# Whole transfers for x and the first weight strip, and the first strip's products by turns of two token tiles

## The reference

```
def first_block(x, pre_mix_w, w_in, ...):
    ...
    h = rmsnorm(x, pre_mix_w[l])
    proj = h @ w_in[l]
    o0 = 0
    q_a = proj[..., o0:o0 + DA_QK] ...
    k_a = proj[..., o0:o0 + DA_QK] ...
```

## Time and profile before

| | |
|---|---|
| median of 3 runs | 753.26 us |
| the profiled execution | 753.9 us |
| its span in the profile | 752.2 us |
| PE busy | 745.2 us, 99% |
| VectorE, ScalarE, GpSimd busy | 480.9, 402.2 and 54.4 us |
| bytes read from memory | 132.61 MB |

### The profile page before, as it was taken

One profiled execution on the slowest core, in us unless ns is written; L12 is line 12 of the kernel. 1 busy time (PEld: TensorE's weight loads), 2 busy tenths in 40 slices (PEclk: granted clock), 3 DMA queues, 4 the chain that ended last, 5 costly groups with the idle time before them and its releaser, 6 DMA issues.

```text
span 752.2 us, 10167 instructions
## 1 busy us (share of the span) xinstructions
PE 745.2 (99%) x3847; PEld 618.6 (82%) x3847; DVE 480.9 (64%) x742; ACT 402.2 (53%) x607; POOL 54.4 (7%) x127
## 2 busy tenths in 40 slices
PE   9999999999999999999999999999999999999997
PEld 7887877888888888888898888888888888888886
DVE  5576766666956665774376877576865575566633
ACT  5646766544744444554368555676345455455422
POOL 1100100000460000000023000200002000000000
PEclk9999999999999999999999999999999999999999
DMA  8855454555656656546476373444464565555541
GB/s 317 269 184 212 137 173 136 191 171 179 220 172 196 192 167 201 196 157 206 127 237 200 110 240 118 126 154 129 147 216 154 190 202 165 193 192 174 195 140 57
DMA packets 57231, 134.34 MB, mean 179 GB/s; under 512 B 7831, under 2 KB 13278, under 8 KB 57182
## 3 DMA queue, kind: packets, MB, share of 16 engines
q1 hardware_dynamic: 56528, 132.16, 54.1%
q10 hardware_dynamic: 654, 1.53, 0.6%
HBM read 132.61 MB, written 1.05 MB: 178 GB/s over the span
## 4 chain that ended last, share of the span: by engine, by line
PE 98%; DMA 1%; DVE 0%; SPq 0%; ACT 0%; POOL 0%; issue 0%; ACTq 0%; POOLq 0%
PE acc L1113 87%; PE aux L1038 4%; PE aux L1216 1%; PE aux L1178 1%; PE aux L1251 1%; DMA x<-in_x_dram 1%; PE aux L1197 1%; PE acc L1104 1%; PE aux L1326 1%; PE aux L1241 0%; PE aux L1104 0%; PE aux L1356 0%; PE aux L1366 0%; PE aux L1341 0%; PE aux L1303 0%; PE aux L1306 0%
## 5 line engine op out<-in xcount | busy, mean ns | idle before, releaser
L1113 PE MATMUL acc<-weights_high,h_high 128*128 128x512 f32 (+1 forms) x720 | 229.3, 394 | 0.0
L1417 DVE SCALAR_TENSOR_TENSOR weights_low<-weights_raw,gain_columns,weights_high 128x1024 fp32r<-128x1024 f32 (+3 forms) x189 | 218.5, 1189 | 15.2 <-ACT weights_high L682 15.1
L1113 PE MATMUL acc<-weights_high,h_low 128*128 128x512 f32 (+1 forms) x720 | 224.3, 387 | 0.0
L1113 PE MATMUL acc<-weights_low,h_high 128*128 128x512 f32 (+1 forms) x720 | 223.9, 387 | 0.0
L682 ACT ACTIVATE weights_high<-weights_raw,gain_columns 128x1024 fp32r<-128x1024 f32 (+3 forms) x188 | 194.6, 1074 | 19.8 <-DMA weights_raw<-in_w_in_dram 11.7
L1113 PEld LDWEIGHTS acc<-weights_low,h_high 128*128 128x128 f32 x720 | 134.4, 188 | 27.6
L1113 PEld LDWEIGHTS acc<-weights_high,h_low 128*128 128x128 f32 x720 | 134.3, 188 | 27.5 <-DVE h_low L1436 0.4
L1113 PEld LDWEIGHTS acc<-weights_high,h_high 128*128 128x128 f32 x720 | 130.7, 188 | 25.4 <-issue 1.9
L1414 DVE TENSOR_TENSOR weights_low<-weights_raw,weights_high 128x1024 fp32r<-128x1024 f32 x68 | 81.0, 1220 | 35.9 <-ACT weights_high L682 35.7
L682 ACT ACTIVATE weights_high<-weights_raw 128x1024 fp32r<-128x1024 f32 x68 | 69.7, 1057 | 48.1 <-DMA weights_raw<-in_ffn_w_down_dram 22.6
L738 ACT ACTIVATE silu_tmp<-acc,stats 128x512 f32<-128x512 f32 (+1 forms) x24 | 15.7, 654 | 88.4 <-PE acc L1113 88.4
(11 more groups left out here) (269 smaller groups left out, 637.4 us busy)
## 6 DMA issues: line engine op xcount, KB each, us to landing
weights_raw<-in_w_in_dram SPq DMA_DIRECT2D x59, 512.0 KB, 5.1
weights_raw<-in_w_gate_dram SPq DMA_DIRECT2D x44, 256.0 KB, 3.4
weights_raw<-in_w_up_dram SPq DMA_DIRECT2D x44, 256.0 KB, 4.0
weights_raw<-in_w_down_dram SPq DMA_DIRECT2D x22, 512.0 KB, 4.6
weights_raw<-in_ffn_w_gate_dram SPq DMA_DIRECT2D x44, 256.0 KB, 3.3
weights_raw<-in_ffn_w_up_dram SPq DMA_DIRECT2D x44, 256.0 KB, 4.1
weights_raw<-in_ffn_w_down_dram SPq DMA_DIRECT2D x22, 512.0 KB, 4.8
weights_raw<-in_w_out_dram SPq DMA_DIRECT2D x16, 512.0 KB, 4.6
```

The source lines that it names most:

```text
L1113: i = nc.tensor.matmul(acc[:, 2 * t + b, 0:width], lhs[:, k0, sl], w[:, u % RING, base + d:base + d + width], start=(kt == 0 and n == 0), ...
L1417: i = nc.vector.scalar_tensor_tensor(lo[:, u % RING, c], raw[:, u % RING, c], gcol[:, g:g + 1], hi[:, u % RING, c].bitcast(F32), ALU.mult, ...
```

## The change

Four edits, all of them in the first microseconds:

- x comes in two transfers of 512 KB, one for each tile, in place of four of 256 KB, and both are issued ahead of strips 1 to 3. Strip 0 comes in one transfer of 512 KB on ScalarE's queue in place of two halves on two queues. ScalarE still makes its high part in two halves.
- The transposes of the identity are 4 in place of 8.
- A new function `first_products` writes the twelve matmuls of strip 0 for both tiles. The list's own steps for them are skipped.
- VectorE makes the high and low part of strips 0 and 1 of tile 0 first (`first_strips(0, 1, "mix_first")`) and those of strips 2 and 3 later, after tile 1's low part (`rest_of_first`).

```diff
-    out.append(do("warm", 8))
-    run("qk_a", [1, 1, 2, 4], {(0, 0): [do("norm_turn", "mix", 1, 0)], ...
+    out.append(do("warm", 4))
+    run("qk_a", [1, 1, 2, 4], {(0, 0): [do("norm_turn", "mix", 1, 0), do("rest_of_first")], ...
...
-            load_x(0, 0)
-            sp.dma_start(raw[:, 0, 512:1024], dram["w_in"][0, 0:P, 512:1024]).then_inc(*tick("raw_loaded0", 0, 16))
-            load_x(1, 0)
+            load_x(0)
+            load_x(1)
             weights(1)
             weights(2)
             weights(3)
-            load_x(0, 1)
-            load_x(1, 1)
...
-            act.dma_start(raw[:, 0, 0:512], ins["w_in"][0, 0:P, 0:512]).then_inc(*tick("first_loaded", None, 16))
+            act.dma_start(raw[:, 0, :], ins["w_in"][0, 0:P, 0:1024]).then_inc(*tick("first_loaded", None, 16))
...
+            def first_products():
+                def passes(t, lhs, w):
+                    for b in range(2):
+                        c = slice(512 * b, 512 * b + 512)
+                        if t == 0 and lhs is hT[0]:
+                            pe.wait_ge(*at("high_ready" if w is hi else "low_ready", (0, 0) if b else "left"))
+                        i = nc.tensor.matmul(acc[:, 2 * t + b, :], lhs[:, 0, t * P:(t + 1) * P], w[:, 0, c],
+                                             start=(lhs is hT[0] and w is hi), stop=False)
+                    return i
+                pe.wait_ge(*at("turned_high_vec", "mix_first"))
+                passes(0, hT[0], hi)
+                pe.wait_ge(*at("turned_low", "mix_first"))
+                passes(0, hT[1], hi)
+                step("norm_turn", "mix", 1, 0)
+                pe.wait_ge(*at("turned_high", ("mix", 1, 0)))
+                passes(1, hT[0], hi)
+                passes(0, hT[0], lo)
+                pe.wait_ge(*at("turned_low", ("mix", 1, 0)))
+                passes(1, hT[1], hi)
+                passes(1, hT[0], lo).then_inc(*tick("weights_used", 0))
...
+            def first_strips(k, bank, key):
+                high, low = (part[:, k:k + 2, 0:P] for part in hT)
+                src = aux[bank][:, 0:2 * P].rearrange("p (k s) -> p k s", k=2)
+                dve.wait_ge(*at("turned", key))
+                signal(nc.vector.tensor_copy(high, src), "turned_high_vec", key, True)
+                nc.vector.tensor_tensor(low, src, high.bitcast(F32), ALU.subtract).then_inc(*tick("turned_low", key))
```

More of the change, by code:

```diff
@@ L219, in timeline @@
     out.append(("ahead", 1))
-    out.append(do("warm", 8))
-    run("qk_a", [1, 1, 2, 4], {(0, 0): [do("norm_turn", "mix", 1, 0)], (0, 2): [do("norm_turn", "mix", 0, 1)],
+    out.append(do("warm", 4))
+    run("qk_a", [1, 1, 2, 4], {(0, 0): [do("norm_turn", "mix", 1, 0), do("rest_of_first")], (0, 2): [do("norm_turn", "mix", 0, 1)],
                             (1, 2): [do("norm_turn", "mix", 1, 1)], (1, 3): [do("stats", "mix", 0)],
@@ L577, in _, with load_x @@
             dram = ins
-            def load_x(t, b):
-                sp.dma_start(x[:, t, 512 * b:512 * b + 512], dram["x"][0, t * P:(t + 1) * P, 512 * b:512 * b + 512])\
-                    .then_inc(*tick(f"x_loaded{t}_{b}", None, 16))
+            def load_x(t):
+                sp.dma_start(x[:, t, :], dram["x"][0, t * P:(t + 1) * P, :]).then_inc(*tick(f"x_loaded{t}", None, 16))
             def bc(ap, n=P):
@@ L671, in advance @@
                             .then_inc(*tick("high_ready", "left"))
-                        act.wait_ge(*at("raw_loaded0", 0))
                         nc.scalar.activation(hi[:, 0, 512:1024], raw[:, 0, 512:1024], ACT.Copy, scale=gcol[:, 0:1])\
@@ L1089, in product @@
                 for n, (lhs, w) in enumerate(passes):
-                    if u == 0 and t == 0 and lhs is xl:
-                        step("norm_turn", "mix", 1, 0)
                     if t == 0 and w is lo:
@@ L1135, in step @@
                         if tag == "mix":
-                            pe.wait_ge(*at(f"x_loaded{t}_{b}"))
+                            pe.wait_ge(*at(f"x_loaded{t}"))
                         elif tag.startswith("merged"):
@@ L1389, in _ @@
             for st in steps:
-                if st == ("do", "norm_turn", "mix", 1, 0):
+                if st in (("do", "norm_turn", "mix", 1, 0), ("mm", "qk_a", 1, 0, None)):
+                    continue
+                if st == ("mm", "qk_a", 0, 0, None):
+                    first_products()
                     continue
@@ L1602, in step @@
                         if (tag, t, b) == ("mix", 0, 0):
[L1603 to L1614, removed]
+                            first_strips(0, 1, "mix_first")
                             continue
@@ L1617, in step @@
                                    0.5 if tag.startswith("merged") else 1.0)
+                elif kind == "rest_of_first":
+                    first_strips(2, 0, ("mix", 0, 0))
                 elif kind == "gain_turn":
```

## The result

The changed kernel takes 757.04 us in the median of 4 runs (756.43 to 758.81), the kernel before 753.25: a ratio of 1.0049, 95% interval 1.0037 to 1.0062. I had forecast 754.4, no change, and a range up to 756.2. The chances had 0.38 on slower, 0.22 of it on the mechanism that turned out to be the largest part.

A forecast was written before the change was run, and what follows sets the result against it. PE, 98% of the chain, was taken to bound the kernel. Landing L = 6.1 plus 5.35 us put strip 1's first product at 11.45 against 10.36, 1.1 us later: 753.26 becomes 754.4 us, range 753.3 to 756.2.

The forecast's parts named there:

- What bounds the kernel: Whole kernel: PE is 98% of the chain, so a change in the opening only moves the start of its gapless streaming.
- The transfers: Opening loads: 1.05 MB instead of 0.79 ahead of the first product; strip 1 taken to land at 9.5 us.
- L: Landing of x tile 0 and strip 0, both whole: taken as 6.1 us, between bounds 5.5 and 7.4.
- rival 1: Opening transfers: bytes come no faster in whole rows, L = 7.4, 2.4 us later, 755.7 us; chance 0.16.
- rival 3: Opening transfers: cold start was a matter of many small packets, L = 5.5, 0.5 us later, 753.8 us; chance 0.14.
- I let it be in by L: Gain columns' row, behind strip 0 on ACT's queue: assumed landed by L, with no time of its own.
- L + 1.45: Opening on PE: the second product's time, after ScalarE makes strip 0's high part in 1.34 us from L.
- From the second product on: Opening on PE: three products, tile 1's transposes and eight more products, to strip 1's first product at L + 5.35.
- VectorE's queue and strip 1's low part: Strip 1's low part, queued behind VectorE's moved pair: 12.43 us against PE's need at 12.37, adding under 0.1 us.
- The clock: Opening on PE: idle from about 4.5 to 6.1 us, then every product at 0.23 us.
- rival 2: Opening on PE: clock rises later after the idle gap, 755.1 to 757.3 us, most likely 755.9; chance 0.22.
- 1.1 us: Strip 1's first product on PE: 11.45 us against 10.36, a delay nothing later takes up.

The follow-up runs named there:

- e6: The changed kernel with the gain row's transfer issued ahead of strip 0's on ScalarE's queue, still 7 zero products: 760.53 us.
- e5: The changed kernel with 11 zero products in place of 7 and the gain row's transfer ahead of strip 0's on ScalarE's queue: 756.41 us.
- e1: The changed kernel with 11 zero products in place of 7 at PE's start: 755.71 us.
- e10: e1 with tile 1's transposes put back ahead of tile 0's activation low pass: 755.26 us.
- e7: e3 with 11 zero products in place of 7 (whole transfers, old order): 755.12 us.
- e9: e1 with the gain row's transfer issued first on SP's queue instead of second on ScalarE's: 755.38 us.
- e12: The old order with the whole transfers, 11 zero products and the gain row first on SP's queue: 754.74 us.
- e2: The kernel before with 3 zero products in place of 7: 755.14 us.
- e3: The kernel before with the whole transfers of x and strip 0 alone: 756.25 us.
- e8: The kernel before with strip 0 whole behind the gain row on ScalarE's queue, x still in halves: 756.23 us.

## Why the prediction was wrong, step by step

- **What bounds the kernel.** Right: the loss lies between the start and strip 1's first product (4.5 of 4.9 us in the profiles); the rest, 0.4 us, is the strip's first products before the clock rose. From 20 us on PE is idle for 5.6 us in all, before and after, and nothing was taken back.
- **The transfers.** Right in the landings, in part by luck. L was 5.8 to 6.0 against 6.1, x tile 1 at 7.3 (7.4), strip 1 at 8.6, better than the 9.5 taken. But the counts of bytes behind these figures are not what the trace has: the prediction let "exactly 1.05 MB" be in at 7.43 us and 0.79 at 5.53, and the queues had moved 1.64 and 0.98 MB by then, because later transfers run beside the earlier ones. In the changed kernel 1.45 MB had moved by 6.0 us, 0.4 more than counted; the higher rate made up for it, 411 in place of 294 GB/s from 4 to 6 us. In that stretch the profiles with whole transfers of x have 408 to 424 GB/s (e6 alone less, 379), and the four with halves 294 to 321. So rival 1, no faster in whole rows, falls, and rival 3's mechanism, a faster opening, is there, though L is 0.3 to 0.5 us over its 5.5. The Trainium skill, "DMA: Bandwidth & Descriptors", has in its section on bandwidth the higher rate of larger loads, and the 411 against 294 GB/s agree. The same page of the Trainium skill has in its section on queues the turns that an engine takes between queues, and the trace agrees: from 3 to 4 us of the changed kernel SP's queue moved 0.18 MB and ScalarE's 0.20, and x tile 0 lands 5.0 us after its issue beside strip 0 and 3.3 us in e5, where it had the engines to itself.
- **"I let it be in by L".** The first step that failed. The gain row stands in ScalarE's queue behind strip 0; before, that was 256 KB and the row was in before PE had ended its zeros; now it is 512 KB at shared engines, and the row lands last, at 6.2 us. ScalarE was to begin at L, but the transposition on PE, VectorE's copy and the hand-overs between the row and ScalarE had no term in the sum: 6.18 to 6.94 is 0.76 us, beside the 0.2 us of the row behind strip 0. In e1 the second product came at 8.40 where L + 1.45 gives 7.5. Size: 0.9 us in the profiles.
- **From the second product on.** 8.40 to 12.21 in e1 is 3.81 us, against 3.90 in the working. The order's cost was in that sum, 0.5 us for the two products ahead of the transposes, but I set it off against the gain at tile 1's low part and never priced the new order on its own. e10 and e7 put it at 0.6 us with whole transfers.
- **VectorE's queue and strip 1's low part.** No wait showed beyond 0.1 us (e1: 13.20 in place of 13.13), as forecast.
- **The clock.** The step that decided. The forecast's sum had PE idle from 4.5 to 6.1 us, the four transposes of x at the lower clock and every product behind them at 0.23 us: it put the pause's effect on the clock at nothing, without a reason. The products took 0.47 us. As rival 2 I gave the late rise 0.22 and called 755.9 most likely; its range, 755.1 to 757.3, holds the median. The matmuls paused for 1.9 us and not 1.6 (the gain row again), and in the profile the clock stayed down to 15.7 us, past all 15 products and transposes that I had counted as the worst case. It costs 3.1 us between the profiled spans, where rival 2's far end was 2.9, and 1.7 us between the medians. The spans of the changed kernel's six executions, 754.7 to 757.2 us, lie 0.7 to 3.2 us over e1's 754.0, so the price differs from one execution to the next.

By medians the 3.8 us are then: 1.7 the clock (e1), about 0.6 the order (e10), about 0.5 the gain row together with strip 0's earlier landing (e9), and 0.9 to 1.0 us left over. These are single differences, taken in different sets; by the intervals of the ratios only the first is clear of the noise, and no run tests the sum. The rest I put down to x tile 0 landing at about 6 us instead of 4.8; e12, 0.9 us above before, has x at 6.45 on its chain, but it also has the zeros ahead of the gain row, so this share isn't shown by itself. My "1.1 us" had been the order and the later landing together.

Open is what sets the instant of the rise. The rise came at 5.9 us (before), between 5.9 and 6.6 (e1), between 10 and 11 (e2), twice at 15.7 (the changed kernel); in e3, e6 and e8 the clock was up, then down, then up. Even with PE at work from 1.10 us without a gap it moved: to about 4.2 us in e7 and e9, to about 6.9 in e5. The zero products' weight loads from 4.5 to 5.0 us, in e7 and in e1:

```profile
L1022 PEld LDWEIGHTS aux<-row 128*128 128x128 f32 x6 | 0.8, 192 | 0.0
```

```profile
L1022 PEld LDWEIGHTS aux<-row 128*128 128x128 f32 x4 | 1.0, 333 | 0.0
```

And e3, whose PE does the same up to 6.4 us as the changed kernel's, pause included, was at the higher clock at 6.4 us and at the lower one from 7.7 to 11. So the program alone doesn't set the instant. Nor do the runs part the first pause from a second one of the changed kernel, 0.7 us ahead of 11.71 while the clock was still low. That a pause in the first microseconds costs time through the clock is shown in both directions, by taking it away (e1) and by putting it in (e2); a rule for how long isn't.

## What to carry to other kernels

Work that nobody reads can be what keeps an engine's clock up: before moving a load that an engine waits for at the start, count the pause that it opens, and fill it, though not for longer than it lasts (e12). Look for the smallest transfer behind the one you enlarge; a 4 KB row queued behind 512 KB landed with it here, and whatever stands between it and its user comes on top. Two queues share the engines, and an issue 0.6 us later cost 1.6 us in e5. And price a new order by itself: whatever stands ahead of the operation that starts the longest chain is on the path.

## What the runs showed of the hardware that I had not expected

- The page's clock row shows 1.00 from 0 to 15 us in the changed kernel while the weight loads take 330 ns in place of 188: durations tell the lower level where the row doesn't. Only after a first rise does the row show 0.50 (e3, e6, e8).
- After a pause of PE's matmuls of 1.9 us, ended at 6.3 us, the profiles of the changed kernel have PE at 1.2 GHz for 9 us more, with one further gap of 0.7 us. In e3 the same pause let it be at 2.4 GHz at 6.4 us, and the clock fell at about 7.7 us, while PE was at work.
- 512 KB from an idle start landed 3.3 us after their issue with the engines to themselves (e5) and 5.0 us beside a second load of the same size on the other queue.
- With PE at work without a gap from 1.10 us on, the first rise of the clock came anywhere from about 4.2 us (e7, e9) to about 6.9 (e5).
